# The delta rule's first stages as one pipeline: decays without a relu, pick buffers and key banks doubled, query products and decays placed late, diagonal blocks gathered before their transpose

## The reference

```python
gcum = jnp.cumsum(g, axis=-1)
decay = jnp.exp(jnp.where(incl, gcum[..., :, None] - gcum[..., None, :], -jnp.inf))
k_beta = k * beta[..., None]
a_kk = jnp.where(strict, jnp.einsum("bhnid,bhnjd->bhnij", k_beta, k) * decay, 0.0)
t_inv = lax.linalg.triangular_solve(eye + a_kk, jnp.broadcast_to(eye, a_kk.shape),
                                    left_side=True, lower=True, unit_diagonal=True)
u = jnp.einsum("bhnij,bhnjd->bhnid", t_inv, v * beta[..., None])
w = jnp.einsum("bhnij,bhnjd->bhnid", t_inv, k_beta * jnp.exp(gcum)[..., None])
qk = jnp.einsum("bhnid,bhnjd->bhnij", q, k) * decay
q_dec = q * jnp.exp(gcum)[..., None]
k_dec = k * jnp.exp(gcum[..., -1:] - gcum)[..., None]

def step(state, inp):
    qd, kd, ui, wi, qki, gt = inp
    v_new = ui - jnp.einsum("bhcd,bhde->bhce", wi, state)
    o = jnp.einsum("bhcd,bhde->bhce", qd, state) + jnp.einsum("bhcj,bhje->bhce", qki, v_new)
    state = state * gt[..., None, None] + jnp.einsum("bhcd,bhce->bhde", kd, v_new)
    return state, o
```

## Time and profile before

| | |
|---|---|
| median of 3 runs | 3796.75 us |
| the 3 runs | 3795.52, 3796.75, 3801.67 us |
| the profiled execution | 3786.07 us |
| its span in the trace | 3784.3 us |
| granted TensorE clock over the span | 0.967 |
| PE busy | 3580.9 us (95%) |
| DVE busy | 1737.4 us (46%) |
| ACT busy | 976.4 us (26%) |
| POOL busy | 1818.5 us (48%) |
| delta rule, layer 0, picks to the zeroing of the output banks | 337.74 to 472.15 us |
| delta rule, layer 1, the same stages | 1320.53 to 1455.11 us |

### The profile page before, as it was taken

The page is one execution under the profiler, slowest core; times in us unless marked ns, Lnnn a source line. Parts: engine busy times, 40 slices in busy tenths (PEclk is TensorE's granted clock), DMA queues, the critical chain, the costliest instruction groups (busy, mean ns, idle before and its releaser), DMA issues.

```text
span 3784.3 us, 49957 instructions
## 1 busy us (share of the span) xinstructions
PE 3580.9 (95%) x18796; PEld 2884.1 (76%) x18796; DVE 1737.4 (46%) x2682; ACT 976.4 (26%) x1724; POOL 1818.5 (48%) x1049
## 2 busy tenths in 40 slices
PE   7999599999999968999999989999999999999999
PEld 5776477888776747787888878788888789888887
DVE  5256644637444583555461164434434124344342
ACT  3235432201223444222111133232101114232110
POOL 5523135666553230566565534436656431535654
PEclk9999699999999969999999989999999999999999
DMA  3210012223221101223232311213322423212322
GB/s 119 85 49 31 1 63 88 93 91 95 93 89 61 51 1 42 75 90 105 83 95 89 94 56 62 67 51 92 106 83 95 111 87 98 78 54 92 100 89 89
DMA packets 80743, 292.88 MB, mean 77 GB/s; under 512 B 8520, under 2 KB 9672, under 8 KB 80456
## 3 DMA queue, kind: packets, MB, share of 16 engines
q1 hardware_dynamic: 78496, 283.82, 23.7%
q10 hardware_dynamic: 1032, 2.62, 0.6%
q0 software_dynamic: 1056, 4.19, 0.4%
HBM read 281.69 MB, written 8.91 MB: 77 GB/s over the span
## 4 chain that ended last, share of the span: by engine, by line
PE 82%; DVE 10%; ACT 3%; issue 3%; DMA 1%; POOL 1%; DVEq 0%; ACTq 0%; SPq 0%; POOLq 0%
PE PSUM L336 20%; PE PSUM L335 20%; PE PSUM L334 20%; PE PSUM L895 2%; PE PSUM L1863 1%; PE PSUM L897 1%; PE PSUM L896 1%; PE PSUM L1867 1%; DVE SLABS L1507 1%; DVE SLABS L1504 1%; DMA SLABS<-w_k 1%; PE PSUM L950 1%; PE PSUM L1441 1%; PE PSUM L907 1%; DVE SLABS L1494 1%
## 5 line engine op out<-in xcount | busy, mean ns | idle before, releaser
L287 POOL TENSOR_TENSOR W_LOS<-SLABS,W_HI 128x1024 fp32r<-128x1024 f32 (+2 forms) x454 | 1158.4, 2552 | 37.8
L285 POOL TENSOR_SCALAR W_HI<-SLABS 128x1024 fp32r<-128x1024 f32 (+2 forms) x454 | 509.4, 1122 | 1313.7 <-DMA SLABS<-w_k 1313.6
L335 PE MATMUL PSUM<-H_LO,W_HI 128*128 128x512 f32 x2480 | 984.3, 397 | 0.0
L334 PE MATMUL PSUM<-H_HI,W_HI 128*128 128x512 f32 x2224 | 884.5, 398 | 26.7 <-DVE H_LO L478 20.6
L336 PE MATMUL PSUM<-H_HI,W_LOS 128*128 128x512 f32 x2224 | 885.5, 398 | 0.0
L335 PEld LDWEIGHTS PSUM<-H_LO,W_HI 128*128 128x128 f32 x2480 | 469.1, 189 | 118.6 <-issue 2.4
L334 PEld LDWEIGHTS PSUM<-H_HI,W_HI 128*128 128x128 f32 x2224 | 419.5, 189 | 132.0 <-issue 22.1
L336 PEld LDWEIGHTS PSUM<-H_HI,W_LOS 128*128 128x128 f32 x2224 | 419.0, 188 | 98.6
L493 DVE TENSOR_TENSOR PSUM<-PSUM,FACTORS 128x512 f32<-128x512 f32 x282 | 195.2, 695 | 555.3 <-PE PSUM L336 493.1
L334 PE MATMUL PSUM<-ACT_HI,W_HI 128*128 128x512 f32 x928 | 369.8, 399 | 8.7 <-DVE H_LO L454 6.4
L336 PE MATMUL PSUM<-ACT_HI,W_LOS 128*128 128x512 f32 x928 | 372.0, 401 | 0.0
(11 more groups left out here) (481 smaller groups left out, 5155.2 us busy)
## 6 DMA issues: line engine op xcount, KB each, us to landing
SLABS<-w_k SPq DMA_DIRECT2D x422, 512.0 KB, 3.5
SLABS<-w_k SPq DMA_DIRECT2D x32, 768.0 KB, 4.2
SLABS<-w_k SPq DMA_DIRECT2D x32, 640.0 KB, 3.9
ARENA<-gate_rows SPq DMA_DIRECT2D x8, 512.0 KB, 5.4
bias_rows<-SQ ACTq DMA_DIRECT2D x1, 2560.0 KB
X<-xT SPq DMA_DIRECT2D x1, 2048.0 KB, 8.6
gate_rows<-RT SPq DMA_DIRECT2D x8, 256.0 KB, 2.1
DX<-bias_rows POOLq DMA_DIRECT2D x8, 256.0 KB, 2.9
```

The costliest lines, as they stand in the source:

```text
L285: nc.gpsimd.tensor_scalar(hi, raw, 1.0, 0.0, MUL, ADD).then_inc(pool_step, 1)
L287: nc.gpsimd.tensor_tensor(lo, raw, hi.bitcast(F), SUB).then_inc(slab_split[s], 1)
L334: mm(out, w_hi, rhs[0](k), start=k == first, stop=False)
L335: mm(out, w_hi, rhs[1](k), start=False, stop=False)
```

## The change

- **No relu.** The Exp reads PSUM directly. Masked entries already hold -1e30; too large values on the other side are cut by DVE later: the key product's instruction becomes a scalar_tensor_tensor with a max, the query product's one with a min.
- **Four pick buffers.** Pairs 2 and 3 have buffers of their own (in H_LO2 and H_HI). DVE builds all its picks at once; ACT keeps its order.
- **Two key banks.** keys(p) uses banks 4, 5 or 6, 7 by turns, and waits for the key multiplication of two pairs before.
- **Late query products.** queries(p) leaves stage 1 for direction 1 of stage 4, as do DVE's multiplications of them, which follow the last inversion. For that, PE's blocks of 64 and 128 use three banks a pair instead of four.
- **Late POOL decays.** The products with the query gains and key decays all follow the last inversion, group by group; the scan waits for its own group's.
- **Gathered blocks.** ACT copies the diagonal blocks of a direction to COMPACT (4 instructions over 32 partitions for pairs 0 to 2, 4 for pair 3; for direction 1, 4 for all pairs), and DVE transposes them with one 128x1024 instruction.
- **TMC before TTC.** The two transposes back change places, each with its own signal.
- Buffers move (states, outer products, gains), with no change in shape.

```diff
-                    nc.scalar.activation(qkd(p, d), pair2(2 * d), ACT.Relu, scale=-1.0).then_inc(dn["relu"], 1)
-                    act.wait_ge(*nth("relu", 2 * p + d + 1))
-                    nc.scalar.activation(qkd(p, d), qkd(p, d), ACT.Exp, scale=-1.0).then_inc(dn["decay"], 1)
+                    nc.scalar.activation(qkd(p, d), pair2(2 * d), ACT.Exp).then_inc(dn["decay"], 1)
...
+            def compact(d, p0, p1):
+                act.wait_ge(*nth("m", 2 * p1 - 1 + d))
+                for c in range(4):
+                    last = nc.scalar.activation(tiles(COMPACT[d], 32)[32 * c:32 * c + 32, 8 * p0:8 * p1, :],
+                                                tiles(MAT[d], 32)[32 * c:32 * c + 32, 8 * p0:8 * p1, 32 * c:32 * c + 32], ACT.Copy)
...
+            compact(0, 0, PAIRS - 1)
             for p in range(PAIRS):
                 last = nc.scalar.activation(QUERY_SQ[p], A(6 + p), ACT.Square)
             last.then_inc(dn["squared"], 1)
+            compact(0, PAIRS - 1, PAIRS).then_inc(dn["diag"], 1)
...
-                for c in range(4):
-                    last = nc.vector.transpose(NA[32 * c:32 * c + 32, :].rearrange("p (i j) -> p i j", j=32),
-                                               tiles(MAT[d], 32)[32 * c:32 * c + 32, :, 32 * c:32 * c + 32].rearrange("p m i -> p i m"))
+                dve.wait_ge(*nth("diag", d + 1))
+                turned_in = nc.vector.transpose(NA.rearrange("p (i j) -> p i j", j=32),
+                                                tiles(COMPACT[d], 32).rearrange("p m i -> p i m"))
...
-                if p:
-                    pe.wait_ge(*nth("m", 2 * p))
...
-                products(p, 4, 10)
+                if p >= 2:
+                    pe.wait_ge(*nth("m", 2 * p - 2))
...
+                products(p, 4 + 2 * (p % 2), 10)
```

More of the change, by code:

```diff
@@ L1251, in delta_act @@
                 for p in range(0, PAIRS, 2):
-                    both = [(4 * d + q, 4 * (q % 2), q) for q in (p, p + 1)]
+                    both = [(4 * d + q, 3 * (q % 2), q) for q in (p, p + 1)]
                     for u, b, q in both:
@@ L1301, in decays @@
                 if p:
-                    pe.wait_ge(*nth("relu", 2 * (p - 1) + d + 1))
+                    pe.wait_ge(*nth("decay", 2 * (p - 1) + d + 1))
                 for hh in range(2):
@@ L1335, in spread @@
                 if i < PAIRS:
-                    pe.wait_ge(*nth("relu", 2 * PAIRS))
+                    pe.wait_ge(*nth("decay", 2 * PAIRS))
                 else:
```

162 lines of the change are left out of this document (86 added, 76 removed).

## The result

| | before | after |
|---|---|---|
| median of 4 runs each | 3796.14 us | 3756.95 us |
| the runs | 3795.43 to 3801.67 | 3755.35 to 3760.46 |
| the profiled execution | 3786.07 | 3760.46 |
| its span | 3784.3 | 3758.6 |

The ratio is 0.9895, with a 95% interval of 0.9879 to 0.9910: 34 to 46 us less.

The account below looks back on a forecast made before the run. PE was taken to bound the kernel, with DVE's share reachable. Layer 0: -14.2 - 5.95 + 3.75 = -16.4; layer 1, 1.3 more: -15.1; together -31.5 us from a median of 3796.75 gives 3765.3 us, range 3751 to 3784.

Parts of the forecast that it names:

- What bounds the kernel: Whole kernel: PE holds 82% of the chain that ended last, DVE 10%, and DVE's share is what the change can reach.
- Stage 1: Up to the first inversion step: ACT's chain sets the end and one gathered transpose replaces four; 14.2 us less per layer.
- The cheap bound for scalar_tensor_tensor: DVE's key multiplication in stage 1: the new instruction costs as much as tensor_tensor, 1.17 us; possibly 10% dearer, without effect.
- the query products in stage 1 lie in none of the chains: Stage 1: moving the query products out of it was counted as no gain, being on neither chain followed there.
- Second direction: Direction 1's inversion: the gathered transpose replaces 7.9 by 1.95 us, 5.95 us less per layer; 1.3 us more in layer 1.
- DVE would be ready 28.65 us after the first, ACT after 26.4: Second hand-over in layer 0: DVE ready later than ACT, so DVE sets it; in layer 1 ACT needs 29.9 us.
- Query products: Direction 1 of stage 4: first call hidden under ACT's block copies, other three counted in full; 3.75 us more per layer.
- the second rival: Direction 1's blocks: query products free because PE's high clock comes earlier, two times 3.75 us back; 3758 us, chance 0.15.
- Late products on POOL: From the last hand-over to the scan: first group 10.4 us against 26.2 + 3.75 us of time, so no cost.
- Low clock in stage 1: Decay and key calls at low clock: 9.65 us later per layer if all; half gives 3775 us, all 3784; chance 0.13.
- A late partner: Scan's head: last query multiplication or POOL's group comes after the blocks, 12 us wait per layer; 3789 us, chance 0.06.
- The scan at low clock: Scan begins at low clock if PE waits at its head; a whole scan low costs 34.5 us per layer, 3834 us; chance 0.04.

Follow-up runs that it names:

- second pair of traces: The kernel before and the changed kernel each run again without edit; medians 3796.93 and 3759.01 us, ratio 0.9900.
- squares_last: Changed kernel with ACT's four query squares placed behind the gathering of pair 3 instead of ahead of it; 3749.1 us, ratio 0.9874 to the kernel before.
- after_again: The changed kernel run once more with no edit; 3759.01 us, ratio 0.9900 to the kernel before.
- queries_out: Changed kernel without the query products of pairs 1 to 3, but for one matrix product each; 3770.2 us, ratio 0.9915 to the kernel before.
- old_buffers: Changed kernel with two sets of pick buffers and one pair of key banks again; 3764.1 us, ratio 0.9927 to the kernel before.
- split_blocks: squares_last with ACT copying only the blocks of the first two pairs before PE may go on; 3755.5 us, ratio 0.9870 to the kernel before.
- before_again: The kernel before the change run once more with no edit; 3796.9 us, ratio 1.0003.
- before_filled: Kernel before the change with three groups of 8 unused products added in direction 1's blocks; 3812.7 us, ratio 1.0050.

## Why the prediction was right, and where it was not

**What bounds the kernel.** Right as far as the stages go: 32.8 and 35.5 us of the gain lie between the picks and the zeroing, and DVE's share of the chain fell from 10% to 9%. In the second pair of traces it fell from 12% to 8%. The medians are further apart; see below.

**Stage 1.** -14.2 us forecast, -14.1 measured in both layers. The mechanism held too: ACT sets the end. Of its terms, the last Exp ended at 362.46 and so 23.2 us after the picks' start, where I had 360.8 - 337.74 = 23.1; the gathering of three pairs took 3.38 (3.3 taken), the squares 2.1 (2.17), the last gathering 1.67 (1.55), the transpose 1.94 (1.95). Interpolating between two shapes of the same copy was enough. PE's part came out by small errors that cancel: the later decay calls took 1.41 to 1.51 us instead of 1.35 and the key calls 1.09 instead of 1.0, but the first call 1.70 instead of 1.9, and the chain began 0.3 us earlier behind the picks. The cheap bound for scalar_tensor_tensor held: 1.17 to 1.22 us, as tensor_tensor. Undoing the parts one by one costs 2.9 (relu), 2.7 (gathering) and 2.8 to 5.9 us (buffers). That is 8.4 to 11.5 of the 14.1, if they add up, which chains that wait for each other need not do. The rest is the late query products and POOL's late products, or comes only with several parts together. Those two were not undone apart, so the forecast's step that the query products in stage 1 lie in none of the chains was not tested.

**Second direction.** -5.95 forecast, -4.7 measured in layer 0. The step that failed is "DVE would be ready 28.65 us after the first, ACT after 26.4". DVE's term was good: squares_last shows 28.9. ACT's was not. I took its length from the kernel before, where the clock came up early in layer 0, although I had the slower case in front of me in layer 1 and used it only there. In the first trace of the changed kernel both layers had the slow course, 29.9 us. The clock of PE in a stretch that was hidden before is part of the price as soon as its cover becomes thin. For layer 1 the number was right, 29.96 us against 29.95, but not because layer 1 is the slow one: in the second trace it is layer 1 that took the quick course, 28.98 us, with ACT waiting for DVE as the step had it. Which layer has which course changes between executions of one program.

**Query products.** +3.75 forecast, +2.4 measured. From the start of each call on the path to the start of what follows it are 1.10, 1.09 and 1.46 us, 3.65 in all, so the calls cost what I had put on them, though it was the last that ran at a lower clock and not the first. What I had at zero are the rows between them. The first transposes took 3.14 us to the next row instead of 3.58, the first 64-wide products 3.82 instead of 4.26, and the second pairs' rows gave 0.17 and 0.20: 1.25 us came back through the clock, a third of what the second rival needed. In layer 1 of after_again it was more: 27.36 - 26.24 = +1.1 us.

**Luck.** In layer 0 the sum came out exactly, -16.4 us. Its last two terms were off by 1.2 us (too much gain) and 1.3 us (too much cost) and cancelled. The measured median of 3756.95 us stands nearer to the second rival's 3758 than to the forecast, but by the rows that rival's mechanism gave only a third of its price there. The lower end of the range was worked out from -42 us, and the terms named for it give 31.5 + 7.5 + 1.1 = 40.1.

**Late products on POOL.** At no cost, as forecast: the memset starts at 427.78, the last product ends at 446.2, and the zeroing comes at 457.25.

**The rivals.** Low clock in stage 1 did not come in the changed kernel: six measurements of this stage, in after, after_again and queries_out, give 32.16 to 32.37 us. It came in old_buffers. A page of the Trainium skill, TensorE: Matmul & The Clock Gate, Part 4 (PE-mode transpose), would have let the decay calls behind the four rounds of transposes begin low. The first bank there did, with 0.70 us near the low pace of 0.73; the next took 0.45. So the clock rose about where the transposes end, and the rival that was drawn from the page did not come. That does not settle the page's rule: decay calls had run until 345.85, just ahead of the transposes, and the profile does not show which mode the transposes ran in. In split_blocks 16 transposes ran in 1.94 us in a stretch with a granted clock of 1.00. A late partner did not come. The scan at low clock came in queries_out only.

**The median.** Here the working does not close. The stages give 32.8 and 35.5 us, the medians 39.2 and 37.9. Both profiled executions of the kernel before (3786.07 and 3788.91 us) lie below its median, and between the profiled executions the difference is only 25.6 and 29.3 us, as the rest of the span was 7.1 and 6.3 us longer in the changed kernel. Whether the change has a part in that is not shown; the medians point the other way. Over 50 runs on two chips the kernel before spreads from 3779.6 to 3810.6 us with a granted clock of 0.962 to 0.970, the changed one over ten runs from 3752.0 to 3761.1 with 0.969 to 0.972.

Part of the gap is in stage 1. In six measurements of the old stage 1 (before, before_again, before_filled, two layers each) the first step comes after 46.43, 46.44, 46.45, 46.46, 47.93 and 51.45 us, a mean of 47.5; the new one has no such spread. By these few that is 1.1 us a layer, or 2 in all, of which the second pair's trace already holds 1.5. The rows show how: PE waits 2.25 us for DVE and is low behind it, and the longer it stays low (one product call, then two, then all of the stage) the later the step. That leaves some 4 us in the first pair and 2 in the second for which I have no place. Applying the profiled execution's distance to the median, as I did, takes it for granted that both kernels have the same distance, and they had not: the kernel before lay 10.1 and 8.0 us below its median, the changed one 3.5 and 0.6 above.

## What to carry to other kernels

Where two engines feed each other in short turns, a second buffer can remove more than the wait that the profile shows, since PE came out of some of these waits at half its clock (behind 2.25 and 1.50 us, but not behind one of 1.85): read the pace of the instructions behind a wait, not the wait alone, and in more than one layer and execution. When a change thins the cover over a stretch, price that stretch at the slowest course that any layer or run shows. When the total of a forecast comes out, check its terms one by one: here two of them were wrong and cancelled. And put the copies that the critical engine waits for ahead of work that nobody waits for, whatever order reads well.

## What the runs showed of the hardware

- Less work on PE can be slower: without the query products, 16 products of the scan took 3.51 instead of 1.89 us, and the first group of the scan 5.8 us more.
- 48 products back to back (11.17 us) did not carry the clock over a later wait of 5.67 us: the products behind it took 1.92 us, as without the filling.
- One program can have its clock rise earlier in one layer than in the other: the changed kernel's stages took 118.0 and 115.7 us in one execution.
- Transposes by PE go with the clock like products: in split_blocks 16 of them took 3.65 us in a stretch with a granted clock of 0.50, 1.94 in one of 1.00.
- A strided copy of 32x512 took 1.09 us on DVE beside POOL and 0.64 on ACT.
- The times of one program lie up to 31 us apart (3779.6 to 3810.6), and go with the mean granted clock of the execution: 0.968 to 0.970 for the seven shortest of the 50, 0.962 to 0.964 for the five longest.
